# A hybrid SSD/S5 decoder step with 32 routed experts: w_out in blocks of 128 columns, a tenth weight buffer, unscaled rows and tile loops by two

## What is computed

```python
x = x + jnp.concatenate([y_ssd, y_s5], axis=-1) @ w_out     # (536, 2048) @ (2048, 1024)
t = _rmsnorm(x, norm_ffn)
lc = t @ rc_w + rc_b ; g_sel = argmax(lc)                   # one of 4 groups of experts
vals, idx = top_k(softmax(lf_sel), 2)                       # two of the 8 experts of the group
for e in range(32):
    h = silu(t @ w_gate[e]) * (t @ w_up[e])                 # 1024 -> 512
    out = out + gates[:, e:e+1] * (h @ w_down[e])           # 512 -> 1024
y = _rmsnorm(x + out, norm_final)
```

## Time and profile before

| | us |
|---|---|
| three runs | 1065.48 median, 1065.2 to 1067.47 |
| the profiled execution | 1063.9 |
| its span, first to last instruction | 1061.9 |
| PE busy in the span | 947.3 (89%) |
| DVE, ACT, POOL busy | 432.0, 329.4, 270.3 |
| HBM read and written | 260.04 MB, 25.41 MB |
| mean granted TensorE clock | 0.968 of full |

### The profile page before, as it was taken

How to read it: one execution, slowest core, us unless ns; L and a number is a source line. 1 busy time by engine, 2 the same in 40 slices (tenths; PEclk the granted TensorE clock), 3 DMA queues, 4 the chain that set the end, 5 groups by cost and what they waited for, 6 DMA issues and landing times. The chain is left out here.

```text
span 1061.9 us, 16825 instructions
## 1 busy us (share of the span) xinstructions
PE 947.3 (89%) x6316; PEld 674.0 (63%) x6317; DVE 432.0 (41%) x739; ACT 329.4 (31%) x662; POOL 270.3 (25%) x510
## 2 busy tenths in 40 slices
PE   6999999999999999999999999988788888778770
PEld 5889779877876789998675555544344444444430
DVE  6999876454557988941611111111010110110112
ACT  3025323453326774322422222221212112122224
POOL 1000888888421010000022222222211111211213
PEclk9999999999999899999999999999998999999995
DMA  7585172111099634264799999999999999999964
GB/s 268 124 143 91 30 121 81 41 62 41 31 251 238 210 123 160 87 267 209 313 324 383 395 391 389 381 398 390 393 412 395 398 413 407 409 417 412 422 250 162
DMA packets 74253, 276.95 MB, mean 261 GB/s; under 512 B 37000, under 2 KB 38920, under 8 KB 57312
## 3 DMA queue, kind: packets, MB, share of 16 engines
q1 hardware_dynamic: 63728, 252.40, 64.9%
q0 software_dynamic: 8720, 19.60, 6.8%
q10 hardware_dynamic: 1760, 4.34, 1.1%
HBM read 260.04 MB, written 25.41 MB: 269 GB/s over the span
## 5 line engine op out<-in xcount | busy, mean ns | idle before, releaser
L658 PE MATMUL ps<-sb_arena 128*128 128x260 f32 (+2 forms) x1152 | 266.3, 393 | 9.5 <-DMA sb_arena<-wi 8.8
L658 PEld LDWEIGHTS ps<-sb_arena 128*128 128x128 f32 x1152 | 220.7, 193 | 55.4 <-DMA sb_arena<-wi 8.6
L1967 DVE TENSOR_TENSOR sb_s5b<-sb_s5b,ps 128x256 f32<-128x256 f32 x34 | 21.1, 622 | 413.0 <-PE ps L1028 413.0
L1028 PE MATMUL ps<-sb_arena 128*64 128x256 f32 x1088 | 134.4, 403 | 32.7 <-DMA sb_arena<-w_up 32.7
L1021 PE MATMUL ps<-sb_arena 128*64 128x256 f32 x1088 | 128.2, 389 | 16.0 <-DMA sb_arena<-w_gate 15.3
L1042 PE MATMUL ps<-sb_arena 128*64 128x512 f32 x544 | 124.2, 598 | 19.9 <-DVE sb_arena L1971 19.9
L1028 PEld LDWEIGHTS ps<-sb_arena 128*64 128x64 f32 x1088 | 82.4, 145 | 82.1 <-DMA sb_arena<-w_up 41.3
L1021 PEld LDWEIGHTS ps<-sb_arena 128*64 128x64 f32 x1088 | 80.5, 140 | 74.0 <-DMA sb_arena<-w_gate 28.7
L1397 ACT ACTIVATE sb_kxf<-ps,sb_gate_of 64x512 f32<-64x512 f32 x36 | 24.6, 682 | 296.2 <-PE ps L1042 295.6
L1042 PEld LDWEIGHTS ps<-sb_arena 128*64 128x64 f32 x544 | 36.9, 136 | 85.4 <-issue 57.5
L1424 DVE TENSOR_TENSOR sb_arena<-sb_arena 128x64 f32<-128x64 f32 (+13 forms) x87 | 78.0, 896 | 17.4 <-DMA sb_arena<-ssm_in 8.2
(11 more groups left out here) (307 smaller groups left out, 1203.3 us busy)
## 6 DMA issues: line engine op xcount, KB each, us to landing
sb_arena<-w_gate SPq DMA_DIRECT2D x32, 2048.0 KB, 42.6
sb_arena<-w_up SPq DMA_DIRECT2D x32, 2048.0 KB
sb_arena<-w_down SPq DMA_DIRECT2D x32, 2048.0 KB, 42.1
sb_arena<-wi SPq DMA_DIRECT2D x28, 512.0 KB, 3.9
sb_arena<-w_out SPq DMA_DIRECT2D x4, 2048.0 KB, 8.4
sb_arena<-ssm_in POOLq DMA_DIRECT2D x8, 512.0 KB, 9.1
sb_arena<-wglu SPq DMA_DIRECT2D x8, 512.0 KB, 5.1
o_ssm_s<-sb_arena POOLq DMA_DIRECT2D x8, 512.0 KB, 4.5
```

Source lines behind the costliest of these rows:

```text
L658: last = mm(ps[:, b0 + h, 0:t1 - t0], ring[w % 3][:, k, :], src[:, k, t0:t1], start=k == 0, stop=k == KD - 1)
L1028: last = mm(ps[64 * r:64 * r + 64, 1, 0:256], xt[:, k, :], Wu[s][:, k, 256 * r:256 * r + 256], start=k == 0, stop=k == KD - 1)
L1967: V.tensor_tensor(hh.rearrange("p (j c) -> p c j", j=2), sg.rearrange("p (c j) -> p c j", j=2), ps[:, 1, 0:256].rearrange("p (c j) -> p c ...
```

## The change

1. **w_out in 16 loads of 128 columns** (0.5 MB each) through three buffers. The high part has a third place for the first nine blocks, and two after that. Load o is asked for when block o - 3 is done. The space of the second 2 MB piece becomes the tenth weight buffer, `Wg_first`, for the gate matrix of expert 0; the `Wg` buffers so hold the gates of experts 1, 2 and 3 at the start and stay one expert ahead.
2. **The S5 root is put on at eviction**: `scale_s5` goes, and `project_out` multiplies all 16 blocks by their root in PSUM. The S5 sums move from block 3 to block 5.
3. **Weight loads are asked for as soon as each buffer's last use is over**: ten before the first tile, in a new order on SP's queue.
4. **Rows are stored unscaled**: ACT no longer writes `xs`; `x_scr` gets `x1` itself, and `sum_scr` is stored from GpSimd's queue at the same time. The root goes into `oh0` for the first tile, and into a new table `root_of` (one DVE operation and ten matmuls more), which is the scale of ACT's copy of the gathered rows. The gathers wait for both stores.
5. **RING = 2**: two gather buffers instead of four, and GpSimd's and ACT's loops turn by two tiles.
6. **The end**: the row tile of 8 rows goes first, and each square is issued ahead of the root of the tile before.

```diff
-RING = 4
+RING = 2
+LAST = (4, 0, 1, 2, 3)
...
-        wo = [part(14944, KD, 512), part(4096, KD, 512)]
+        wo = [part(14944 + 1024 * i, KD, P) for i in range(3)]
+        Wg_first = part(4096, KD, FF)
+        hi_of = [o % 3 if o < 9 else (o + 1) % 2 for o in range(16)]
...
+            sp.wait_ge(hn_done, NS)
+            sp.dma_start(Wu[1], usrc[1]).then_inc(wu_ld[1], 16)
+            def next_wo(o):
+                sp.wait_ge(o_mm, o - 2)
+                wo_load(o)
+            next_wo(3)
             sp.wait_ge(y2_done, 8)
-            sp.wait_ge(wide_done, NW)
-            wo_load(1)
-            sp.wait_ge(o_mm, 4)
-            wo_load(2)
+            sp.dma_start(Wg_first, gsrc[0]).then_inc(ld_x[0], 16)
+            for o in range(4, 7):
+                next_wo(o)
...
-            sp.wait_ge(o_mm, 8)
-            wo_load(3)
-            sp.dma_start(Wg[0], gsrc[0]).then_inc(wg_ld[0], 16)
-            sp.dma_start(Wg[2], gsrc[2]).then_inc(wg_ld[2], 16)
-            sp.wait_ge(o_mm, 12)
+            for o in range(7, 11):
+                next_wo(o)
             sp.dma_start(Wu[0], usrc[0]).then_inc(wu_ld[0], 16)
+            next_wo(11)
+            next_wo(12)
+            sp.dma_start(Wg[0], gsrc[1]).then_inc(wg_ld[0], 16)
+            next_wo(13)
+            next_wo(14)
             sp.dma_start(Wd_to[0], dsrc[0]).then_inc(wd_ld[0], 16)
+            next_wo(15)
+            sp.dma_start(Wg[2], gsrc[3]).then_inc(wg_ld[2], 16)
+            sp.wait_ge(o_mm, 16)
+            sp.dma_start(Wd_to[1], dsrc[1]).then_inc(wd_ld[1], 16)
+            sp.dma_start(Wg[1], gsrc[2]).then_inc(wg_ld[1], 16)
             sp.dma_start(Wu[2], usrc[2]).then_inc(wu_ld[2], 16)
...
-            sp.wait_ge(xs_st, 80)
-            for i, (t0, n) in enumerate(TR):
-                sp.dma_start(sum_scr[t0:t0 + n, :], x1[i][0:n]).then_inc(sum_st, 16)
-            sp.wait_ge(xtr, 2)
+            sp.wait_ge(x1t_mm, 9)
             sp.dma_start(Wd_to[2], dsrc[2]).then_inc(wd_ld[2], 16)
...
+            pl.wait_ge(x1t_ev, 10)
+            for i, (t0, n) in enumerate(TR):
+                pl.dma_start(sum_scr[t0:t0 + n, :], x1[i][0:n]).then_inc(sum_st, 16)
             pl.wait_ge(tab_ev, 1)
             pl.wait_ge(xs_st, 80)
-            for u in (1, 2, 3, 0):
+            pl.wait_ge(sum_st, 80)
+            for u in (1, 0):
...
+            for j in range(10):
+                last = mm(ps[0:T, 5, T:T + IDXC], oh_row[:, j, :], oh_root[:, j, :], start=j == 0, stop=j == 9)
...
-                act_(xs[i][0:n], x1[i][0:n], ACT.Copy, scale=ssum[0:n, i:i + 1]).then_inc(xs_done, 1)
-                ac.wait_ge(xs_done, i + 1)
-                ac.dma_start(x_scr[t0:t0 + n, :], xs[i][0:n, :]).then_inc(xs_st, 16)
+                ac.dma_start(x_scr[t0:t0 + n, :], x1[i][0:n, :]).then_inc(xs_st, 16)
...
             ac.wait_ge(x1t_mm, 10)
+            ac.wait_ge(oh_done, 2)
             act_(first[:, 0:512], ps[0:64, 4, :], ACT.Copy).then_inc(x1t_ev, 1)
...
-                    act_(xst, xg[(u + 1) % RING], ACT.Copy).then_inc(staged, 1)
+                    act_(xst, xg[(u + 1) % RING], ACT.Copy, scale=root_of[:, bass.ds(q + 1, 1)]).then_inc(staged, 1)
...
-                if q < 2:
-                    if o:
-                        dv.wait_ge(o_ev, o)
-                    tt(pair(sqx), src, pair(root_b[0]), ALU.mult)
-                    src = pair(sqx)
+                tt(src, src, pair(root_b[o // 8]), ALU.mult)
...
-            V.tensor_tensor(oh0, both[:, :, 0], both[:, :, 1], ALU.add).then_inc(hot_done, 1)
+            tt(oh0, both[:, :, 0], both[:, :, 1], ALU.add)
+            V.tensor_tensor(oh0, oh0, bc(ssum[:], 2, T), ALU.mult).then_inc(hot_done, 1)
...
+            tt(oh_root.rearrange("p (i k) t -> p i (k t)", k=2), oh_tile.rearrange("p (i k) t -> p i (k t)", k=2),
+               bc(ssum[:], 2, 2 * IDXC), ALU.mult)
```

More of the change, by code:

```diff
@@ L191, in build @@
         Wd_to = [part(o + 8192, 2, 2 * D) for o in W_off]
-        xg = [part(4288 + 1024 * i, D, p=(0, T)) for i in range(RING)]
+        Wg_first = part(4096, KD, FF)
+        xg = [part(1024 * i, D, p=(0, T)) for i in range(RING)]
         xst = part(8384, D, p=(0, T))
@@ L195, in build @@
         ht = part(9920, 2, P)
-        Lt = part(4288, NT, p=(0, 36))
-        xs = [part(o, D) for o in (4824, 5848, 6872, 19040, 20064)]
-        first = part(21088, D, p=(0, T))
+        Lt = part(9806, NT, p=(0, 36))
+        first = xst
+        root_of = part(10176, IDXC, p=(0, T))
         g8 = part(10344, KD)
-        rt = [8208]
+        rt = [8192]
         def small(*shape):
@@ L933, in _ @@
             pe.wait_ge(root_in, 2)
-            project_block(3, sums=1)
-            for o in range(4, 8):
-                project_block(o)
+            project_block(3)
+            project_block(4)
+            project_block(5, sums=1)
+            project_block(6)
+            project_block(7)
             for o in range(8, 12):
@@ L1308, in _ @@
             root_wide(0)
-            for k in range(4, KD):
-                ac.wait_ge(y2_done, k + 1)
-                square(1, sig, k)
             ac.wait_ge(hn_done, NS)
@@ L1798, in _ @@
                 sample_update(b)
[L1799 removed]
+            low_parts(0, ySSD, PF_GSSD, range(KD))
             gate_product(2)
@@ L1807, in _ @@
             gate_product(7)
-            sum_first(1)
+            wo_low(2)
             root_inverse(0)
@@ L1835, in _ @@
             project_out(0)
+            sum_first(1)
             project_out(1)
+            wo_low(3)
             sum_second(1)
-            wo_low(1)
             project_out(2)
+            wo_low(4)
+            low_parts(1, sig, PF_GS5, range(4))
+            project_out(3)
+            wo_low(5)
+            low_parts(1, sig, PF_GS5, range(4, KD))
+            project_out(4)
+            wo_low(6)
+            project_out(5)
+            wo_low(7)
             root_square(1)
-            project_out(3)
+            project_out(6)
+            wo_low(8)
+            project_out(7)
+            wo_low(9)
             root_inverse(1)
-            scale_s5(0)
-            project_out(4)
-            scale_s5(1)
-            low_parts(1, sig, PF_GS5)
-            project_out(5)
-            wo_low(2)
-            project_out(6)
-            project_out(7)
             project_out(8)
+            wo_low(10)
             dv.wait_ge(moe_ld, 64)
@@ L1863, in _ @@
             project_out(9)
-            wo_low(3)
+            wo_low(11)
             for d in range(1, 6):
                 project_out(9 + d)
+                if d <= 4:
+                    wo_low(11 + d)
                 x1_sum(d)
```

177 lines of the change are left out of this document (100 added, 77 removed).

## The result

The changed kernel takes 1081.64 us in the median of its first four runs (1072.88 to 1083.06), the kernel before 1065.34: a ratio of 1.0141 on record, with an interval of 1.0078 to 1.0204. So it is slower, by 16.3 us and then 13.6 us between the medians, and above the range that was given. The profiled execution is the quickest of the first four, 1072.88 us with a span of 1071.0, so what the trace can account for is 9.1 us; the rest of the 16.3 is seen in no trace.

What follows compares the result with a forecast made beforehand. PE bounds the projection, weights the tiles. +0.9 us at the last up matrix and -6.3 behind it make -5.4: 1058.5 against the profiled 1063.9, predicted as 1060 on the runs' scale; forecast's range 1055 to 1065, whole 1052 to 1072.

Steps and rivals of the forecast that it cites:

- Projection: Projection stage: 0 change, since the matmuls are the same and PE fills the stage; bounds -1 to +6.
- Routing: Before the first tile: added DVE operations and ten table matmuls delay the first gate matmul by 2.9 us; bounds +0.5 and +5.
- First gather: Start of the tiles: gathers wait for stores landing by 541.4, rows wanted at about 545; +1 us, bounds 0 and 5.
- The requests after it need no new cover: SP's queue: after the first refill request, later weight requests wait for nothing new, being asked for as buffers come free.
- +4.5 through a hole in the flow: Early tiles: two gather buffers free weight buffers later, leaving a weight-flow hole near the second two-tile expert; bounds 0 and 12.
- 27.8 for two tiles, 13.9 a tile: Tiles: sum of the two-buffer ring's links from gather to scatter, below the weights' 15.6 us per tile.
- Its waits could cost clock besides ... so I add nothing: Tiles: PE's waits on the gather ring might lower its granted clock; priced at nothing.
- the gather ring sets the pace: Rival, tiles: the ring decides the last output; at p (mean us per tile) = 15, 1048.6 and time 1074.7; chance 0.17.
- Ten matrices, -10.0 and +6.4: Weight flow: 86 matrices left instead of 88 saves 10.0 us; a later first refill costs 4.4 and about 2.
- The end, -6.3: After the last output: both empty GpSimd rounds go, SP's stores end the program at 1055.6 instead of 1061.9; bounds 0, -8.
- +0.9 forecast: At the last up matrix: the sum of -10.0, +4.4, +2 and +4.5 us.
- 10.9 us of pauses in the flow (4.4, 2 and 4.5): Weight flow: later first refill 4.4 us, idle engines delivering again about 2, hole from two gather buffers 4.5.

Runs made afterwards that it cites:

- Run 2: The changed kernel, with up matrix 2 and down matrix 2 asked for only when the stores to sum_scr have landed: 1068.53 us.
- Run 1: The changed kernel with four gather buffers again (RING = 4): 1067.56 us.
- run 9: The changed kernel with three extra, unused 128x256 matmuls on PE per tile, ahead of the transposes that wait for the row copy: 1076.24 us.
- run 3: The changed kernel with RING = 4 and the stores of rows ahead of the last two matrices: 1058.48 us.
- run 7: The changed kernel with two buffers, next gather ahead of the scatter wait, stores ahead of two matrices, and nine matrices in hand instead of ten: 1055.03 us.
- Runs 3 and 6: 6 is the changed kernel with two buffers, next gather ahead of the scatter wait, and stores ahead of two matrices: 1055.89 us.
- run 5: The changed kernel with RING = 2, the next gather asked for ahead of the wait for the scatter's landing: 1060.80 us.
- run 11: The changed kernel once more, unedited: 1078.23 us, ratio 1.0148.

## Why the prediction was wrong

**Projection: right.** 106.02 of 107 us busy.

**Routing: a little high.** The first gate matmul comes at 535.9 against 534.2, +1.7 for the +2.9 forecast.

**First gather, "I take 1, bounds 0 and 5": wrong.** The stores landed at 542.8, for the 541.4 worked out. But the step compared this landing with the time at which the rows are wanted, and left out the gather itself, which the same text prices at 8.4 us. The gather is issued at 543.74; 1.0 of issue and 8.6 to the copy make 553.4, and the wait is 11.56. Tile 0's output ends 13.7 later than before (563.43 against 549.71), for +3.9 forecast. From it follows what the text denied with "The requests after it need no new cover": the first refill was asked for at 543.30, for 545.1 forecast, but the second stood behind tile 0's down product until 561.95, and from 545 to 580 the DMA engines lost 10.9 us. Run 2 gives 8.7 us back at the last output.

**RING = 2, "+4.5 through a hole in the flow": right in its mechanism, low in size.** The hole came near 670 as forecast, at 0.72 of DMA share over 30 us: 8.7 us for 4.5. Run 1, which takes the ring away, brings the last up matrix from 1039.0 to 1027.5 and the last output 12.0 us forward. Part of the size is the ring's period, "27.8 for two tiles, 13.9 a tile". In the turn shown above its links are: scatter 8.7 (8.85 forecast); its landing to the next gather's issue 1.3 (1.01); rows copied 9.5 after that (8.4); copy to transposes 1.3 (1.06); transposes to the output's end 832.87 - 824.18 = 8.7 (7.14); output to scatter 1.3 (1.23): 30.75. The link that is wrong in kind is the fifth. It holds the down product, which runs right behind PE's wait at a lower granted clock: 5.22 for 3.65. The text said "Its waits could cost clock besides ... so I add nothing", because the waits for weights in the late stretch had left the clock at 1.00. Those waits lie ahead of gate and up products, outside any ring. The 25.2 us of slow down products behind tile 0 are 0.76 a tile, and 14.76 - 0.76 = 14.0 is close to the 13.9 of the sum. Of the 25.2, the 8.1 before 760 us fall where later buffers can leave the DMA engines idle; how much of the hole they make is not shown. The 17.1 after that made no difference at the end that run 9 could tell.

By the Trainium skill (TensorE: Matmul & The Clock Gate, Part 1) activity holds the clock up and idle time lets it fall; the trace agrees, with a granted clock of 0.69 behind the wait of 3.41 us and 26.6 / 16 = 1.7 us lost on a slow down product. The text cited it and gave it no price.

**The rival "the gather ring sets the pace": half right, and its number near by luck.** PE does wait on the ring in nearly every pair of tiles to the end. But the rival took it that either the ring or the weights decide. Here the ring starved the weights early, and at the end both were equally late. Its 1048.6 for the last output at p = 15 is close to the measured 1050.4, with p at 14.76 and a tile 0 that ends 9.8 later than its formula has it.

**Ten matrices, -10.0 and +6.4: the first about twice too large.** With ring and first gather mended (run 3) the last up matrix comes 5.1 earlier; the two terms together said 3.6. But for the tenth matrix alone 5 had been counted, and run 7 shows no such gain. From 509 to 545 the DMA engines are busy 0.90 of the time in the changed kernel, 0.89 in the kernel before. So by this reading only what is loaded during the projection counts, and that is one matrix more, not two: before had asked for five by 508, the change for six.

**The end, -6.3: right in its cause, -8.2 in size.** GpSimd's last instruction, a drain of 6.6 us that the profile doesn't count as work, began at 1055.06 in the kernel before and ended the program; it now starts at 1055.59, beside SP's loads and stores, and ends 6 us before their last one is issued. Runs 3 and 6 differ in it by 8.1.

Taken together on the profiled executions: at the last up matrix +16.7, for +0.9 forecast. The forecast had 10.9 us of pauses in the flow (4.4, 2 and 4.5), and 21.5 were lost from 545 to 760; it had 10.0 for the matrices in hand, and some 5 are left between the 21.5 and the 16.7. The ring adds 0.6 behind the last up matrix, and the end takes off 8.2: +9.1.

## What to carry to other kernels

Write down a ring of waits link by link before a buffer is taken out of it, and price each PE product in it that stands directly behind a wait at the lower clock as well as at the full one. Then ask what a slower ring starves: here it cost little by itself, and much by letting the DMA engines stand early, which they could not make good later. Ask first whether a landing needs to be waited for where it is: here one wait moved behind the next request made two buffers do the work of four, with the shorter end besides (run 5, 1060.8 us for the changed kernel's 1078.2 to 1081.6). Once the DMA engines are full, another buffer in hand bought nothing that could be told here, and a store that someone waits for belongs ahead of the loads that nobody needs yet.

## What was not expected of the hardware

- 50 us of extra matmuls in the tiles cost no time that can be told: 1076.24 us against 1078.23 without them. In every second tile they lie where PE waited before, and the granted clock is 0.99 instead of 0.93 from 760 to 1000.
- The length of the pause alone does not tell whether the down product is slow: in the changed kernel 0.87 us of wait (at 924.80) were followed by 3.65 us, 1.35 us (at 910.07) by 4.88; in run 2 0.57 us (at 632.04) by 5.31, and in run 11 2.26 us (at 925.54) by 3.65.
- Beside a full flow of weights a gather lands 6.3 to 9.7 us after the start of its issue, but three that were issued when the flow paused or thinned out (555.60, 636.80 and 679.42) already after 3.8 to 4.5.
